# Norm sums by a ones matrix, unit 1's weights in tiles of their own, scaled chunks in PSUM, low parts on GpSimd, squares added in pairs

## The chip, the cores and the metric

One core of a Trainium2 chip. The metric is the device time of one launch in microseconds, median of three runs.

## The reference

A decoder of three layers on one sequence of 512 tokens with 1024 features, in float32. What the change touches is the sequence of RMS norms between the parts:

```python
mixed = jnp.concatenate([y, m_out], axis=-1) @ w_out[l]
h = h + rms_norm(mixed, norm_mix_post[l])
f = swiglu_ffn(rms_norm(h, norm_ffn_pre[l]), w_ffn_in[l], w_ffn_out[l])
h = h + rms_norm(f, norm_ffn_post[l])
```

for l = 0 and 1 (after layer 0's feed-forward `rms_norm(h, norm_kv)` feeds the keys and values). `rms_norm(x, g)` is `x * rsqrt(mean(x * x) + 1e-6) * g`, with the mean over the 1024 features. A third layer follows: a recurrent and Fourier mixer, a post norm, and a mixture of 16 experts.

## The kernel before

The residual stream X lies in SBUF as 8 chunks of 128 features by 512 tokens. A product in float32 is made as three passes in a reduced float32 format: weights and activations are split into a high part (a copy that rounds) and a low part (the difference), and `three_pass` issues high x high, high x low and low x high, each a matmul with 512 columns. `stream` walks over units of two halves (s = 0, 1) of 128 x 1024 weights: SP loads a half into `ring[s]`, ScalarE makes its high part (`split_high`, L221), VectorE the low part (`split_low`, L227), TensorE multiplies. A slot s of `wh`/`wl` is free when the product that read it is done (`used_done`). Rings 2 and 3 carry the modulation weights that GpSimd's queue loads (L189) and VectorE sums up beside the feed-forward (L263).

A layer's output product (`rows_products`) collects all 8 output chunks in the 8 PSUM banks, bank c for chunk c; in its last half TensorE ends them one by one. `rows_root` copies bank 0 to SBUF (`kept`), squares the chunks on ScalarE, adds six of the squares on VectorE, sums over the partitions by matmuls with one column of ones (four token blocks for each of three parts, `roots[:, 0, 0:4]`), takes root and reciprocal of 128 x 4, and spreads the result over the partitions again (`spread_passes`, L525) into bank 0. The first weights of the next product are split on the way. A feed-forward's output lacks one factor, the root of the norm in front of it; so behind a feed-forward the small constant under the root is replaced by a 128 x 4 tile made from that norm's sums (`root_floor`).

`Residual.chunks` then runs over the 8 chunks: VectorE scales chunk k out of its bank (`scale`), adds it to X, ScalarE makes the high part of the next norm's input (times `next_gain`, without its root) and the square, VectorE the low part, and TensorE multiplies the chunk with unit 0 of the next weights (`one_pass`, L654, banks 0 and 1), and sums the square over the partitions by four one-column matmuls (`sum_tokens`). `stream(fused=...)` calls this in place of unit 0; then unit 1's weights are split into the same two slots, `fused.root()` takes the root, unit 1 is multiplied, `fused.spread()` spreads the root to `rstd_t` behind its first half, and the units are evacuated with it. Engines run their own queues in program order; `Queue.do` (L69) issues an instruction that counts its line up, so L69 stands for most of them in the profile.

The chain occurs at five seams: mixer output to feed-forward in layers 0 and 1, layer 0's feed-forward to keys and values (all three with a fused unit 0), layer 1's feed-forward to the norm of the third layer (`norm2`), and the third layer's mixer output to its norm (`norm3`).

## Time and profile before

| | |
|---|---|
| runs | 1956.45, 1950.61, 1950.71 us |
| median | 1950.71 us |
| profiled execution: first to last instruction (span) | 1947.3 us |
| mean granted TensorE clock | 0.950 |
| TensorE busy | 1814.3 us (93%) |
| VectorE busy | 1216.2 us (62%) |
| ScalarE busy | 896.1 us (46%) |
| GpSimd busy | 125.7 us (6%) |
| chain that ended last | PE 85%, DVE 7%, ACT 6% |

Busy is the time in which an engine works on something; the span is the profiled execution's own time between its first and its last instruction, and what lies around it is not in the trace. The granted clock is 1.0 at 2.4 GHz and 0.5 at 1.2 GHz. The chain is followed back from the last instruction to what released each step.

### The profile page before, as it was taken

To read this page: it belongs to the slowest core of one execution; us is meant where nothing else is said; L and a number is where in the kernel's file an instruction comes from. 1 tells how busy PE (TensorE), PEld (TensorE's weight loads), DVE (VectorE), ACT (ScalarE), POOL (GpSimd) and SP (SyncE) were. 2 spreads that over 40 slices of the span, in tenths; PEclk is the share of its full clock that TensorE was granted. 3 is DMA by queue.
4 is the path that set the end of the run, shared out by engine and by line. 5 is a ranking of instruction groups with operands and counts; after the bars stand their busy time and mean duration, and the time that the engine had idled before them with its cause. 6 is when DMAs were issued, how large, how long until landed. Compare 5 with 4: busy or idle time off the path is not lost.

```text
span 1947.3 us, 25641 instructions
## 1 busy us (share of the span) xinstructions
PE 1814.3 (93%) x9201; PEld 1507.9 (77%) x9201; DVE 1216.2 (62%) x2170; ACT 896.1 (46%) x1452; POOL 125.7 (6%) x137
## 2 busy tenths in 40 slices
PE   7997999999999997899999999799987989999997
PEld 7875788888887865678888888678576878888885
DVE  3554668887323656456865532564575479889888
ACT  3446443222213445543223221342383368888885
POOL 1000000000000000000110000120000210110102
PEclk8898999999999998999999999799998879999999
DMA  4223225455333124024655423330011359999995
GB/s 150 87 76 115 87 64 142 134 145 147 107 96 96 44 65 184 23 65 137 182 159 149 119 93 97 112 89 22 21 67 66 108 222 377 395 385 370 386 372 187
DMA packets 203854, 289.32 MB, mean 149 GB/s; under 512 B 12332, under 2 KB 150548, under 8 KB 203636
## 3 DMA queue, kind: packets, MB, share of 16 engines
q1 hardware_dynamic: 188788, 239.56, 36.9%
q0 software_dynamic: 11920, 36.48, 6.1%
q10 hardware_dynamic: 3056, 12.06, 1.6%
q8 instruction: 59, 0.97, 0.2%
q14 instruction: 31, 0.25, 0.0%
HBM read 271.77 MB, written 21.53 MB: 151 GB/s over the span
## 4 chain that ended last, share of the span: by engine, by line
PE 85%; DVE 7%; ACT 6%; issue 1%; DMA 1%; POOL 0%; DVEq 0%; ACTq 0%; POOLq 0%
PE bank L200 23%; PE bank L202 23%; PE bank L201 23%; PE bank L69 11%; PE bank L654 2%; DVE weights_low L227 1%; PE bank L2195 1%; ACT weights_high L221 1%; DVE tmp L69 1%; DVE z_and_u L69 1%; DVE ring L69 1%; PE bank L1651 1%; ACT spare L69 1%; PE bank L2544 1%; PE bank L272 1%
## 5 line engine op out<-in xcount | busy, mean ns | idle before, releaser
L227 DVE TENSOR_TENSOR weights_low<-ring,weights_high 128x1024 fp32r<-128x1024 f32 x202 | 246.7, 1223 | 395.3 <-ACT weights_high L221 394.8
L200 PE MATMUL bank<-XH,weights_high 128*128 128x512 f32 x1056 | 423.2, 401 | 17.8 <-DVE weights_low L227 6.5
L202 PE MATMUL bank<-XH,weights_low 128*128 128x512 f32 x1056 | 415.6, 394 | 0.0
L201 PE MATMUL bank<-XL,weights_high 128*128 128x512 f32 x1056 | 415.2, 393 | 0.0
L221 ACT CAST weights_high<-ring 128x1024 fp32r<-128x1024 f32 x202 | 211.1, 1047 | 432.6 <-PE bank L202 422.8
L200 PEld LDWEIGHTS bank<-XH,weights_high 128*128 128x128 f32 x1056 | 200.8, 190 | 63.0 <-DVE weights_low L227 9.6
L202 PEld LDWEIGHTS bank<-XH,weights_low 128*128 128x128 f32 x1056 | 200.7, 190 | 43.4
L201 PEld LDWEIGHTS bank<-XL,weights_high 128*128 128x128 f32 x1056 | 201.1, 190 | 40.3 <-issue 0.5
L2235 DVE TENSOR_TENSOR XL<-ring,XH 128x1024 fp32r<-128x1024 f32 x144 | 169.8, 1219 | 11.7 <-ACT XH L2229 11.7
L2229 ACT CAST XH<-ring 128x1024 fp32r<-128x1024 f32 x144 | 145.2, 1048 | 0.6 <-PE bank L202 0.6
L69 DVE SCALAR_TENSOR_TENSOR squares<-ring,c_silu,squares 128x128 f32<-128x128 f32 x384 | 135.2, 352 | 13.6
L200 PE MATMUL bank<-hidden_high,weights_high 128*128 128x512 f32 x352 | 137.1, 390 | 0.0
L202 PE MATMUL bank<-hidden_high,weights_low 128*128 128x512 f32 x352 | 137.0, 389 | 0.0
L201 PE MATMUL bank<-hidden_low,weights_high 128*128 128x512 f32 x352 | 136.9, 389 | 0.0
L189 POOL DMA_DIRECT2D ring<-in_w_ada x48 | 42.5, 885 | 711.9 <-DVE squares L263 711.9
L2235 DVE TENSOR_TENSOR weights_low<-ring,weights_high 128x1024 fp32r<-128x1024 f32 x72 | 86.0, 1216 | 0.0
L1196 ACT ACTIVATE tmp<-tmp 128x512 f32<-128x512 f32 x44 | 27.8, 632 | 109.2 <-DVE tmp L1192 109.1
L202 PEld LDWEIGHTS bank<-hidden_high,weights_low 128*128 128x128 f32 x352 | 66.1, 188 | 13.8
L201 PEld LDWEIGHTS bank<-hidden_low,weights_high 128*128 128x128 f32 x352 | 66.1, 188 | 13.8
L200 PEld LDWEIGHTS bank<-hidden_high,weights_high 128*128 128x128 f32 x352 | 66.1, 188 | 13.4
L200 PE MATMUL bank<-weights_high,gathered_high 128*128 128x256 f32 (+1 forms) x216 | 70.8, 328 | 3.6 <-DVE weights_low L2235 1.8
L2229 ACT CAST weights_high<-ring 128x1024 fp32r<-128x1024 f32 x72 | 74.1, 1053 | 0.0
(506 smaller groups left out, 3263.2 us busy)
## 6 DMA issues: line engine op xcount, KB each, us to landing
ring<-in_w_ffn_in SPq DMA_DIRECT2D x88, 512.0 KB, 4.7
ring<-in_w_gate SPq DMA_DIRECT2D x72, 512.0 KB, 5.4
ring<-in_w_up SPq DMA_DIRECT2D x72, 512.0 KB, 7.3
ring<-in_w_down SPq DMA_DIRECT2D x72, 512.0 KB, 5.9
ring<-in_w_ada POOLq DMA_DIRECT2D x48, 512.0 KB, 4.7
ring<-in_w_ffn_out SPq DMA_DIRECT2D x44, 512.0 KB, 3.6
ring<-in_w_out SPq DMA_DIRECT2D x24, 512.0 KB, 3.6
slot_output<-expert_out SPq DMA_DIRECT2D x18, 512.0 KB, 6.7
```

The lines of the kernel that those rows point to most:

```text
L69: op(*args, **kw).then_inc(self.line.sem, 1)
L189: queue.eng.dma_start(dst, src).then_inc(ln.sem, 16)
L200: PE.matmul(out_ap, w_h, x_h, start=first, stop=False, skip_group_check=True)
L201: PE.matmul(out_ap, w_h, x_l, start=False, stop=False, skip_group_check=True)
L202: return PE.matmul(out_ap, w_l, x_h, start=False, stop=last, skip_group_check=True)
L221: S.copy(wh[:, s, :], ring[s][:, :]).then_inc(high_done.sem, 1)
L227: V.tensor_tensor(wl[:, s, :], ring[s][:, :], wh[:, s, :].bitcast(F32), ALU.subtract).then_inc(split_done.sem, 1)
L272: t = PE.matmul(bank[7][:, 2 * n + j:2 * n + j + 1], ada_acc(n, j), ones[:, 0:1], start=True, stop=True, skip_group_check=True)
L654: return PE.matmul(bank[s][:, cols], w[:, s, k * P:(k + 1) * P], x[:, k, cols], start=start, stop=stop, skip_group_check=True)
L1196: S.activation(sg, sg, ACT.Silu).then_inc(silu_done.sem, 1)
L2229: S.copy(high[s], raw[q]).then_inc(l_high.sem, 1)
L2235: V.tensor_tensor(low[s], raw[q], high[s].bitcast(F32), ALU.subtract).then_inc(l_split.sem, 1)
```

## The change

1. `rows_root` sums each of its three parts with one matmul of 128 x 128 ones by 512 columns, so that every partition of bank 0 holds the sum; root and reciprocal are taken of 128 x 512 into `rstd_t`; the spreading is gone. The floor of a feed-forward output is no longer a 128 x 4 tile but a 128 x 512 part (in `spare`) that enters VectorE's chain of additions as one more term. Both splits of the next weights' first halves stand in `rows_root` right behind their high parts.
2. `Early`: unit 1's weights of each feed-forward are loaded into rings 2 and 3 during the mixer output before, and split into tiles of their own. The first modulation loads of each feed-forward move behind that. In `stream`, unit 1 reads those tiles, and unit 2's halves are split in place of unit 1's while unit 1 is multiplied. Waits on slots name the slot's own split.
3. `Transition` replaces `Residual` at the three fused seams: scaled chunks from chunk 2 on are written back to their PSUM bank; squares of odd chunks go to `spare` or to PSUM, VectorE adds each to the even chunk's square, and four sums (ones matrix, or by token at the keys' seam) take the place of eight; the low parts of chunks 0, 1, 2, 4, 5 and 6 are made by a whole copy on ScalarE and a subtraction on GpSimd; TensorE multiplies the low part of a chunk behind the high part of the next. Its root is of 128 x 512 (by token at the keys' seam).

The core of the diff:

```diff
+        class Early:
+            def load(self, *after):
+                sp.need(*after)
+                for s in range(2):
+                    ap, view = self.src(self.unit, s)
+                    load(sp, landed[2 + s], view(ring[2 + s][:, :]), ap)
+
+            def split(self, s, *after):
+                act.need(*after)
+                S.wait_ge(landed[2 + s].sem, landed[2 + s].n)
+                S.copy(self.high[:, s, :], ring[2 + s][:, :]).then_inc(self.high_line.sem, 1)
+                self.high_line.n += 1
+                V.wait_ge(self.high_line.sem, self.high_line.n)
+                V.tensor_tensor(self.low[:, s, :], ring[2 + s][:, :], self.high[:, s, :].bitcast(F32),
+                                ALU.subtract).then_inc(self.split_line.sem, 1)
...
                     elif fused and i == 1:
                         if s == 0:
-                            fill_half(src, i, 0)
-                            fill_half(src, i, 1)
+                            if not early:
+                                fill_half(src, i, 0)
+                                fill_half(src, i, 1)
                             fused.root()
...
+                    elif early and i == 1:
+                        PE.wait_ge(early.split_line.sem, s + 1)
+                        products(i, s, False, early).then_inc(used_done.sem, 1)
...
                             for both in range(2):
+                                if early:
+                                    open_half(src, both, 2)
                                 evacuate(0, both, used_done.n - 2)
...
-            squares = (sq[:, 0, :], sq[:, 1, :], tmp[:, 0, :], spare[:, 1, :])
+            base, used, total = chunk_done.n - (KC - 1), used_done.n, spare[:, 1, :]
+            squares = (sq[:, 0, :], sq[:, 1, :], tmp[:, 0, :], tmp[:, 1, :])
...
+                if c == 0 and floor:
+                    added[c] = vec.do(V.tensor_tensor, total, total, squares[0], ALU.add, after=[squared[0]])
...
-                for t in range(TT):
-                    tok = pe.do(PE.matmul, bank[0][:, t:t + 1], part[:, t * P:(t + 1) * P], ones[:, 0:1],
-                                start=n + t == 0, stop=n == 2, skip_group_check=True)
...
+                tok = pe.do(PE.matmul, bank[0][:, :], ones[:, :], part, start=n == 0, stop=n == 2, after=[ready])
+            bias = {} if floor else {"bias": epsilon[:, 0:1]}
+            t = act.do(S.activation, rstd_t[:, :], bank[0][:, :], ACT.Sqrt, scale=1.0 / D, after=[tok], **bias)
             bank_free[0] = [t]
...
-            return spread_passes(0, 0, t)
+            return vec.do(V.reciprocal, rstd_t[:, :], rstd_t[:, :], after=[t])
...
+                def square(k):
+                    dst = second[k] if k % 2 else sq[:, k // 2 % 2, :]
+                    squared[k] = act.do(S.activation, dst, X[:, k, :], ACT.Square,
+                                        after=[*x_ready[k], *([summed[k - 4]] if k in (4, 6) else [])])
+
+                def pair(k):
+                    paired[k] = vec.do(V.tensor_tensor, sq[:, k // 2 % 2, :], sq[:, k // 2 % 2, :], second[k + 1], ALU.add,
+                                       after=[squared[k], squared[k + 1]])
...
+                def lows(k):
+                    if k in (3, last):
+                        V.wait_ge(act.line.sem, high[k][1])
+                        low[k] = vec.do(V.scalar_tensor_tensor, XL[:, k, :], X[:, k, :], self.next_gain[:, k:k + 1],
+                                        XH[:, k, :].bitcast(F32), ALU.mult, ALU.subtract)
+                    else:
+                        whole = whole_of[k % 4]
+                        act.do(S.activation, whole, X[:, k, :], ACT.Copy, scale=self.next_gain[:, k:k + 1],
+                               after=[low[k - 4]] if k >= 4 else [])
+                        G.wait_ge(act.line.sem, act.line.n)
+                        low[k] = pool.do(G.tensor_tensor, XL[:, k, :], whole, XH[:, k, :].bitcast(F32), ALU.subtract)
...
+                for k in range(1, KC):
+                    if k < last:
+                        scale(k + 1)
+                    add(k)
+                    highs(k)
+                    lows(k)
+                    square(k)
+                    if k % 2:
+                        pair(k - 1)
+                    PE.wait_ge(act.line.sem, high[k][1])
+                    for s in range(2):
+                        one_pass(s, wh, XH, k)
+                        one_pass(s, wl, XH, k)
+                    if k < last:
+                        pe.need(low[k - 1])
+                        for s in range(2):
+                            one_pass(s, wh, XL, k - 1)
+                        if k in (3, 5):
+                            sums(k - 3)
+                sums(last - 3)
+                for s in range(2):
+                    for k in (last - 1, last):
+                        pe.need(low[k])
+                        done = one_pass(s, wh, XL, k, stop=k == last)
+                    done.then_inc(used_done.sem, 1)
+                slots_used(0, 1)
+                sums(last - 1)
...
+            if i == 3:
+                early.split(s, used_done.now())
...
+        early = Early("first_ffn", ffn_src(0), 1, unit_high, unit_low)
+        early.load(used_done.now())
+        rooted = mix_out(I["w_out"][0], ffn_src(0), row_order, row_ready, row_part)
+        G.wait_ge(early.split_line.sem, 2)
         modulation_load(0)
         modulation_load(1)
...
+        def split_early(i, s):
+            if i == 2:
+                early.split(s, used_done.now())
```

## Rows read from the trace of the kernel before

**Rows 1.** The page: the engine TensorE, and the chain that ended last.

```profile
PE 1814.3 (93%) x9201; PEld 1507.9 (77%) x9201; DVE 1216.2 (62%) x2170; ACT 896.1 (46%) x1452; POOL 125.7 (6%) x137
...
PE 85%; DVE 7%; ACT 6%; issue 1%; DMA 1%; POOL 0%; DVEq 0%; ACTq 0%; POOLq 0%
```

**Rows 2.** Windows: length, busy time of each engine, TensorE's clock, DMA.

```profile
262.70:277.30 14.60, 13.79 (x57) 11.03 (x57) 4.90 (x8) 4.29 (x7) 0.00 (x0) 0.88 0.26 73
270.70:276.18 5.48, 5.48 (x27) 4.41 (x25) 2.31 (x4) 4.08 (x5) 0.00 (x0) 1.00 0.01 3
```

**Rows 3.** Timeline of TensorE at the first seam: start, length, instruction, idle before.

```profile
235.62 1.31 PE L69 MATMUL bank<-ones,tmp 128*128 128x1 f32 x8
237.58 2.05 PE L69 MATMUL bank<-const_tables,roots 128*128 128x128 f32 x8 [0.66 <-DVE roots L69]
241.98 0.55 PE L654 MATMUL bank<-XH,weights_high 128*128 128x256 f32 x1 [2.34 <-DVE tmp L69]
```

**Rows 4.** Timeline of VectorE at the first seam.

```profile
239.67 0.75 DVE L69 SCALAR_TENSOR_TENSOR tmp<-spare,columns,bank 128x512 f32<-128x512 f32 x1 [1.12 <-PE bank L69]
```

**Rows 5.** Timelines of TensorE and VectorE at seams B and D.

```profile
625.76 1.03 PE L69 MATMUL bank<-ones,tmp 128*128 128x1 f32 x8
...
628.75 0.75 DVE L69 SCALAR_TENSOR_TENSOR tmp<-spare,columns,bank 128x512 f32<-128x512 f32 x1 [0.20 <-PE bank L69]
...
1241.74 1.03 PE L69 MATMUL bank<-ones,tmp 128*128 128x1 f32 x8
...
1245.66 0.75 DVE L69 SCALAR_TENSOR_TENSOR tmp<-spare,columns,bank 128x512 f32<-128x512 f32 x1 [1.12 <-PE bank L69]
```

**Rows 6.** Timeline of one chunk inside unit 0 of the first seam.

```profile
252.69 0.74 DVE L69 SCALAR_TENSOR_TENSOR tmp<-bank,columns,rstd 128x512 f32<-128x512 f32 x1
...
252.81 0.72 ACT L69 ACTIVATE XH<-X,columns 128x512 fp32r<-128x512 f32 x1 [0.90 <-DVE X L69]
...
253.44 0.61 ACT L69 ACTIVATE spare<-X 128x512 f32<-128x512 f32 x1
253.56 0.75 DVE L69 SCALAR_TENSOR_TENSOR XL<-X,columns,XH 128x512 fp32r<-128x512 f32 x1
...
254.23 0.68 DVE L69 TENSOR_TENSOR X<-X,tmp 128x512 f32<-128x512 f32 x1
...
254.84 0.74 DVE L69 SCALAR_TENSOR_TENSOR tmp<-bank,columns,rstd 128x512 f32<-128x512 f32 x1
```

**Rows 7.** Timeline of TensorE: first products of units 1 and 2 in A, values in B.

```profile
262.71 0.50 PE L200 MATMUL bank<-XH,weights_high 128*128 128x512 f32 x1 [0.31 <-DVE weights_low L227]
...
277.23 0.50 PE L200 MATMUL bank<-XH,weights_high 128*128 128x512 f32 x1 [0.81 <-DVE weights_low L227]
...
653.26 0.55 PE L200 MATMUL bank<-weights_high,XH 128*128 128x256 f32 x1 [1.76 <-DVE weights_low L227]
```

**Rows 8.** Groups by form: busy us, mean ns of one, idle before, releaser.

```profile
L69 DVE RECIPROCAL swa_small<-swa_small 128x4 f32<-128x4 f32 x12 | 2.1, 178 | 0.4
...
L69 DVE RECIPROCAL mem_small<-mem_small 128x4 f32<-128x4 f32 x8 | 1.4, 171 | 0.0
L69 DVE TENSOR_SCALAR mem_small<-mem_small 128x4 f32<-128x4 f32 x8 | 1.4, 170 | 0.3
...
L69 DVE RECIPROCAL out_root<-out_root 128x1 f32<-128x1 f32 x4 | 0.7, 164 | 1.3 <-ACT out_root L69 1.3
...
L69 DVE TENSOR_TENSOR bank<-bank,const_tables 128x512 f32<-128x512 f32 x8 | 5.6, 695 | 10.5 <-PE bank L69 10.5
...
L69 POOL TENSOR_TENSOR squares<-squares 128x512 f32<-128x512 f32 x2 | 3.4, 1708 | 162.8 <-ACT squares L69 162.8
...
L2647 PE MATMUL bank<-ring,const_tables 128*128 128x512 f32 x16 | 7.5, 592 | 0.0
```

**Rows 9.** Timeline of ScalarE at the end of the first mixer output.

```profile
228.39 1.05 ACT L221 CAST weights_high<-ring 128x1024 fp32r<-128x1024 f32 x1 [4.39 <-PE bank L202]
```

**Rows 10.** Timeline of VectorE at seam D, with GpSimd adding.

```profile
1250.62 0.98 DVE L69 TENSOR_TENSOR X<-X,tmp 128x512 f32<-128x512 f32 x1
```

**Rows 11.** Windows in the attention of layer 1, columns as in rows 2.

```profile
764.00:768.00 4.00, 2.34 (x18) 1.54 (x16) 3.93 (x19) 3.61 (x13) 0.00 (x0) 1.00 0.00 0
768.70:772.00 3.30, 3.30 (x32) 3.28 (x32) 1.06 (x4) 2.29 (x10) 0.00 (x0) 0.50 0.00 0
```

More of the change, by code:

```diff
@@ L229, in split_low, with slots_used, wait_slots, __init__ @@
             split_done.n += 1
+            slot_split[s] = split_done.n
+        def slots_used(*each):
+            for s in each:
+                used_done.n += 1
+                slot_used[s] = used_done.n
+        def wait_slots(*each):
+            PE.wait_ge(split_done.sem, max(slot_split[s] for s in each))
+        class Early:
+            def __init__(self, name, src, unit, high, low):
+                self.src, self.unit, self.high, self.low = src, unit, high, low
+                self.high_line, self.split_line = line(f"{name}_high_done"), line(f"{name}_split_done")
+            def load(self, *after):
[11 more added lines that the diff above has]
+                                ALU.subtract).then_inc(self.split_line.sem, 1)
+                self.split_line.n += 1
         def fill_half(src, i, s):
@@ L288, in opener, with stream @@
             return lambda s: open_half(src, s)
-        def stream(units, src, products, evacuate=None, side=None, then=None, fused=None, beside=None, paired=None):
+        def stream(units, src, products, evacuate=None, side=None, then=None, fused=None, beside=None, paired=None, early=None):
             pending = []
@@ L338, in stream @@
                             pending.append(n)
-                            if n + 2 < 48:
+                            if n + 2 < 48 and n + 2 not in (20, 21):
                                 modulation_load(n + 2)
@@ L379, in columns_products, with products @@
         def columns_products(n, xh, xl, to=0, ready=None):
-            def products(i, s, first):
-                w_h = wh[:, s, :].rearrange("p (k n) -> p k n", k=KC)
-                w_l = wl[:, s, :].rearrange("p (k n) -> p k n", k=KC)
+            def products(i, s, first, halves=None):
+                high, low = (halves.high, halves.low) if halves else (wh, wl)
+                w_h = high[:, s, :].rearrange("p (k n) -> p k n", k=KC)
+                w_l = low[:, s, :].rearrange("p (k n) -> p k n", k=KC)
                 b = to + 4 * (i % 2) + s
@@ L393, in columns_products, with token_products @@
             return products
-        def token_products(tiles, xh, xl, to=0, between=None):
+        def token_products(tiles, xh, xl, to=0, between=None, early=None):
             for a in range((tiles + 1) // 2):
                 pe.need(*bank_free[to + a])
-            PE.wait_ge(split_done.sem, used_done.n + 2)
+            if early:
+                PE.wait_ge(early.split_line.sem, 2)
+            else:
+                wait_slots(0, 1)
+            w_h, w_l = (early.high, early.low) if early else (wh, wl)
             for m in range(tiles):
@@ L409, in token_products @@
             last.then_inc(used_done.sem, 2)
-            used_done.n += 2
+            if early:
+                used_done.n += 2
+            else:
+                slots_used(0, 1)
         def rows_products(units, xh, xl, ready=None, order=None, tokens=None, between=None):
@@ L599, in chunks @@
             def chunks(self):
-                order = range(KC)
                 squares = (sq[:, 0, :], sq[:, 1, :], spare[:, 1, :])
-                scaled, summed, low, squared, routed, paired = {}, {}, {}, {}, {}, {}
-                pairs = self.router is None and self.next_gain is None
+                scaled, summed, squared, routed, paired = {}, {}, {}, {}, {}
+                pairs = self.router is None
                 square = [squares[h] for h in ((0, 1, 2, 1, 0, 1, 2, 1) if pairs else (0, 1, 2, 0, 1, 2, 0, 1))]
@@ L621, in token_sums @@
+                    if j:
+                        bank_free[j] = [scaled[j]]
                 def token_sums(src, first):
@@ L635, in sum_tokens @@
                             summed[j] = token_sums(square[j], False)
-                    elif not self.router:
-                        pe.need(squared[j])
-                        summed[j] = token_sums(square[j], j == 0)
                     else:
@@ L734, in root @@
                            bias=epsilon[:, 0:1], after=[self.summed])
-                if self.keep_floor:
-                    t = vec.do(V.tensor_scalar, root_floor[:, :], bank[2][:, 0:TT], EPS / D, EPS * EPS, ALU.mult, ALU.add,
-                               after=[t])
                 bank_free[2] = [t]
@@ L1460, in program @@
         row_ready = {c: outputs_done[5] for c in range(KC)}
-        spread = mix_out(I["w_out"][1], ffn_src(1), row_order, row_ready)
+        unit_high, unit_low = (QL[:, 4 * n:4 * n + 4, :].rearrange("p c t -> p (c t)").rearrange("p (s n) -> p s n", s=2)
+                               for n in range(2))
+        early = Early("second_ffn", ffn_src(1), 1, unit_high, unit_low)
+        early.load(used_done.now(), (ada_summed, ada_sums[19]))
+        def split_early(i, s):
+            if i == 2:
+                early.split(s, used_done.now())
+        root_table()
+        rooted = mix_out(I["w_out"][1], ffn_src(1), row_order, row_ready, split_early)
+        G.wait_ge(early.split_line.sem, 2)
+        modulation_load(20)
+        modulation_load(21)
         b_ctx.close()
```

236 lines of the change are left out of this document (120 added, 116 removed).

## The prediction

> **What bounds the kernel now.** I read the page first: TensorE sets 85% of the chain that ended last, over a span of 1947.3 us [rows 1]. So the change pays only where TensorE stands idle, runs at half clock, or does work that can go. I call the seams that it touches A (mixer output to first feed-forward, from 233.7 us), B (first feed-forward to keys, 623.9), C (mixer output to second feed-forward, 852.8), D (second feed-forward to the norm behind it, 1239.8) and E (last mixer output, 1535.2). Everything outside them is the same code.
>
> Then the windows: in A the second fused unit (unit 1) takes 14.5 us at a mean clock of 0.88, though the 24 passes that start in a stretch of 5.48 us at full clock need 0.228 us each [rows 2]. 48 passes would be 10.95 us, so unit 1 loses about 3.6 us, 1.75 of them by the clock (0.12 of 14.6). The timeline shows the idle time ahead of unit 0: the last token sum ends at 236.93, the eight small spreading passes run from 237.58 to 239.63, and the first product starts at 241.98 [rows 3]; between these VectorE scales chunk 0 from 239.67 [rows 4] and chunk 1 behind it, and the product waits for the latter. In B and D the sums end at 626.79 and 1242.77 and chunk 0 is scaled at 628.75 and 1245.66 [rows 5]; C behaves as B (1.88 us), E too (1.89), D as A (2.89, the spreading at half clock). Inside unit 0 (20.73 us in A, from 241.98 to 262.71 [rows 3, 7]), VectorE scales a chunk every 2.15 us and ScalarE makes high part and square between [rows 6]: both are nearly as full as TensorE. Behind it come waits for split weights: 0.31 us before unit 1, 0.81 before unit 2, and 1.76 behind unit 0 of B [rows 7].
>
> The sum is made against the span of 1947.3 us; the median of the runs is 1950.71, so 3.4 us lie outside it and are carried over.
>
> **1. Root on all 512 columns (five seams).** The 12 one-column matmuls become three of 512 columns. One of those is two records; sixteen records of such a form have a mean of 592 ns [rows 8] and start 0.43 us apart, so 0.86 us a part against 0.88 now: no change. Root, reciprocal of 4, spreading go; a root of 512 comes (0.60, as a square of 512 columns takes 0.61 [rows 6]), a reciprocal of 512 and 0.15 us of handovers. The reciprocal of 512 has no row. Below, it is a plain pass of 512, 0.69 us. Above, I take the slope from 164 ns for one column to 178 for four (swa_small), 4.7 ns a column: 2.55 us. I take 0.70, since on the same tile four columns cost 171 ns as a reciprocal and 170 as a tensor_scalar [rows 8], which leaves no room for several cycles per column. So from end of sums to chunk 0: 1.45 us, against 2.74 (A), 1.96, 1.88, 2.89, 1.89: gain 1.29 + 0.51 + 0.43 + 1.44 + 0.44 = 4.1 us. The page VectorE: DVE Perf Modes of the Trainium skill (the 8-slice pipeline) says that reciprocal runs divide steps with a repeat count of 8; read as eight cycles an element at its 0.96 GHz that is an estimate of 4.3 us for 512 columns, and the change would then come out about 18 us worse than by my value. The row of four columns speaks against that reading. After feed-forwards (B, D) one more addition heads VectorE's chain of sums; the total is then ready at about 625.75, when TensorE comes free of the second part at 625.7, so it costs nothing, but has no slack left.
>
> **2. Weights split early.** Unit 1 has its own tiles, split during the mixer output, a stage that TensorE sets. SP issues the two loads before the mixer rows, in place of two loads that GpSimd issued then: the same bytes, so I cost it at nothing. In C both splits end well before the seam. In A the second one waits, at i = 3, for the product before last, that is until 228.39, the very moment when the root's first split starts now [rows 9]. Behind it on ScalarE stand that split (1.05 us) and the squares, and on VectorE its low part (1.22) stands before the copy of bank 0 and so before the whole chain of additions. Followed through with those durations, chunk 7's square ends 1 us later than now and the sums at 237.7 instead of 236.93. Cost 0.8 us, in A alone; if the slack were better than I think, 0.
>
> **3. Unit 0 rewritten (A, B, C).** VectorE loses six low parts (0.67 between starts each), gains four pair sums. ScalarE gains six copies of 0.72. GpSimd makes six low parts at 1.7 us [rows 8], less than the time between chunks, so they hide; uncovered, each would cost its 1.7. TensorE drops four of eight token-sum groups. But the order on the queues couples two engines. VectorE's pair sum of an odd chunk waits for that chunk's square, the last of ScalarE's three works, and the next scale and addition stand behind it; ScalarE meanwhile has nothing. A work is followed by the next 0.63 us after its start when it is a high part or a whole copy (252.81 to 253.44 [rows 6]), and about 0.54 when it is a square. With t from the first product: addition 1 ends at 1.3, square 1 at 3.2, then pair, scale, addition: addition 2 ends at 5.2. Chunks 2 and 3 end their squares at 8.25 and the low part of 3 at 8.55, addition 4 ends at 10.4, square 5 at 14.1, addition 6 at 16.1, high part 7 at 18.65. TensorE then still has four passes, a 512-wide sum, four passes, a last sum: 0.9 + 0.86 + 0.9 + 0.86, so 22.25. TensorE's own work (48 passes, four sums: 14.4 us at full clock) fits in it. Writing scaled chunks to PSUM is free: VectorE from bank to bank is 695 ns [rows 8]. While GpSimd adds, VectorE's additions of two SBUF tiles take 0.98 us, not 0.69 [rows 10]; pair 0 and low part 3 meet this on the path: 0.3 each. Unit 0 comes to 22.85 us, between 20.7 (the present length, if the coupling hid) and 24.5 (half clock in the tail, whose 3.5 us would double in part).
> Now: 20.73 in A (from 241.98 to 262.71) and as much in C (20.63); loss 2.1 and 2.2. In B unit 0 and the wait behind it are 22.2 now. The splits of the value weights start when half 0's last pass ends; the token sum between the halves goes, so that this pass comes about 0.6 us closer to the end, and the wait of 1.76 us [rows 7] becomes about 2.25: 22.85 + 2.25, loss 2.9. Sum: 7.2 us lost.
>
> **4. Unit 1.** With weights ready and no spreading passes, unit 1 can run its 48 passes in 10.95 us, and unit 2's weights are split by 8.1 us after its start. Against 14.5 now, gain 3.56 in A and in C: 7.1 us. This needs full clock. Now unit 1 has 0.88 in the mean, behind a tail of one-column sums; the new tail is 3.5 us of wide work. If the clock falls anyway I lose 1.7 us a seam.
>
> **Sum.** -4.1 + 0.8 + 7.2 - 7.1 = -3.2 us: span 1944.1, median **1947.5 us**.
>
> **Rivals.**
> - *Reciprocal slow.* 1.85 us more in each of five seams, 9.3 us: 1956.8, slower. It decides once the reciprocal costs over 1.35 us, where the sum is nought. For it: the growth from one to four columns; against: the two equal rows. 0.13.
> - *Clock falls inside unit 0.* TensorE is busy about 60% of the time from t = 10 to t = 18. In attention, 4 us at 2.34 busy stood at clock 1.00 and were followed by 3.3 us at 0.50 [rows 11]. A fall here would put tail or unit 1 at half clock in A, B, C: 3 x 1.7 = 5.1: 1952.6, no change. 0.24.
> - *The coupling hides.* If square and pair sum overlap more than the order suggests, unit 0 keeps its 20.7 us or less: 2.15 us back in each, 6.4 us: 1941.1, faster. For it: the sum of ScalarE's work is only 14.5 us in all. 0.22.
> - *No effect*, i.e. unit 1 again waits, for its root instead: then about 1951, 0.05.
> - My forecast with its own neighbourhood, 1945 to 1950: 0.36.
>
> A measurement of this kernel can tell 0.3%, 5.9 us. The forecast lies inside it, and so do the clock and the no-effect case in the main: same 0.45. Faster (the hidden coupling and the lower edge of the forecast) 0.32; slower (reciprocal, or clock and long unit 0 together) 0.23. The range goes from 1940.5 to 1957; the forecast's own is 1944 to 1951.
>
> **What would show it.** A 512-wide reciprocal of about 0.7 us, and chunk 0 scaled 1.45 us behind the sums. In unit 0, gaps of about 2 us in ScalarE before the high parts of chunks 2, 4 and 6, each ended by VectorE, and unit 0 two microseconds longer. No wait in front of units 1 and 2 of A and C. In B a wait of 2.2 us for weights_low. In A squares that start 1.6 us later. I am wrong if the reciprocal is long, if the granted clock is half at the end of unit 0, or if GpSimd's low parts take over 2.5 us and TensorE waits for them.

## The result: 1970.2 us, 1% slower, and the profile after

The changed kernel takes 1970.2 us (median of 4 runs, 1968.5 to 1973.6), the kernel before beside it 1950.97 (4 runs). The ratio is 1.0094, 95% interval 1.007 to 1.0118: slower, outside my range of 1940.5 to 1957. The execution that was profiled is the slowest of the four (1973.6).

The page of the changed kernel, engines and chain, against [rows 1]:

```profile
PE 1804.8 (92%) x8911; PEld 1471.9 (75%) x8911; DVE 1235.9 (63%) x2164; ACT 904.0 (46%) x1463; POOL 150.5 (8%) x155
...
PE 81%; DVE 9%; ACT 7%; issue 2%; DMA 1%; POOL 0%; ACTq 0%; DVEq 0%; POOLq 0%
```

TensorE works 9.5 us less, and yet the span is 24.8 us longer (1972.1): VectorE's share of the chain went from 7% to 9%, TensorE's from 85% to 81%. The group of the reciprocals by form: five are those of `rows_root`, two those of `Transition`'s own root in A and C. Below it, VectorE at seam A, against [rows 4]:

```profile
L69 DVE RECIPROCAL rstd<-rstd 128x512 f32<-128x512 f32 x7 | 23.5, 3353 | 12.3 <-ACT rstd L69 12.3
```

```profile
240.86 3.35 DVE L69 RECIPROCAL rstd<-rstd 128x512 f32<-128x512 f32 x1 [0.91 <-ACT rstd L69]
244.25 0.75 DVE L69 SCALAR_TENSOR_TENSOR tmp<-spare,columns,rstd 128x512 f32<-128x512 f32 x1
...
249.83 1.28 DVE L69 TENSOR_TENSOR squares<-squares,spare 128x512 f32<-128x512 f32 x1 [1.99 <-ACT spare L69]
...
270.31 3.35 DVE L69 RECIPROCAL rstd<-rstd 128x512 f32<-128x512 f32 x1 [3.26 <-ACT rstd L69]
```

TensorE at the same seam, against [rows 3, 7] (last part of the sums, first product of unit 0, last sum, first product of units 1 and 2):

```profile
239.08 1.02 PE L69 MATMUL bank<-spare,ones 128*128 128x512 f32 x2
...
246.68 0.55 PE L783 MATMUL bank<-XH,weights_high 128*128 128x256 f32 x1 [6.58 <-DVE tmp L69]
...
268.54 1.02 PE L69 MATMUL bank<-squares,ones 128*128 128x512 f32 x2
268.99 0.80 PE L200 MATMUL bank<-XH,next_unit_high 128*128 128x512 f32 x1
...
280.59 0.39 PE L200 MATMUL bank<-XH,weights_high 128*128 128x512 f32 x1
```

The reciprocal of 512 columns is 3.353 us, not 0.70: the wait before the first product went from 2.34 to 6.58 us. Units 0 and 1 together went from 35.25 us (241.98 to 277.23) to 33.91, and no wait stands in front of units 1 and 2 any more: the second reciprocal of A (270.31) runs beside unit 1 and costs nothing there.

Both profiled executions, cut at the same instructions, give this table: length now minus length before, in us, and what the prediction's steps say of it.

| stage | measured | predicted |
|---|---|---|
| start to the mixer's last projection scaled out before A (same code) | +2.45 | 0 |
| A: from there to the end of sums | +0.72 | +0.8 |
| end of sums to first product, A / B / C | +1.53 / +2.22 / +2.40 | -1.29 / -0.51 / -0.43 |
| end of sums to chunk 0, D / E | +1.17 / +2.25 | -1.44 / -0.44 |
| first product to first modulation sum, A / C | -1.50 / -1.36 | -1.46 / -1.36 |
| B: first product to values | +4.28 | +2.9 |
| B: values to next projections | +1.14 | 0 |
| both feed-forward output products | +3.48, +3.48 | 0 |
| attention (same code) | -2.12 | 0 |
| experts to the last root | +2.74 | 0 |
| the rest | +1.95 | 0 |

The first line is the clock: TensorE's matmuls step at full clock from 24.9 us on before and from 34.1 on now, in code that the change does not touch; a part of that is made up again by 73 us, where the kernel before is at half clock for longer. The rows of the chunks' coupling come out as forecast in A and C, not in B. The roots are each 2.6 to 2.8 us worse than forecast. And 9.7 us lie in the two output products and the experts' stage, of which the prediction does not speak. ScalarE inside unit 0 of A:

```profile
249.11 0.61 ACT L69 ACTIVATE spare<-X 128x512 f32<-128x512 f32 x1
252.40 0.72 ACT L69 ACTIVATE XH<-X,columns 128x512 fp32r<-128x512 f32 x1 [2.68 <-DVE X L69]
...
257.55 0.72 ACT L69 ACTIVATE XH<-X,columns 128x512 fp32r<-128x512 f32 x1 [2.19 <-DVE X L69]
...
263.20 0.72 ACT L69 ACTIVATE XH<-X,columns 128x512 fp32r<-128x512 f32 x1 [2.08 <-DVE X L69]
```

Three gaps of 2.1 to 2.7 us before the high parts of chunks 2, 4 and 6, each ended by VectorE, which itself had waited for ScalarE's square (1.99 us at 249.83).

The feed-forward output products are the same instructions in both kernels, in the same order, at clock 1.00, with no wait. First and last of 71 successive matmuls before (70 steps in 15.86 us: 0.2266 us), TensorE's timeline:

```profile
607.63 0.39 PE L201 MATMUL bank<-hidden_low,weights_high 128*128 128x512 f32 x1
...
623.49 0.39 PE L202 MATMUL bank<-hidden_high,weights_low 128*128 128x512 f32 x1
```

and of 78 in the changed kernel (77 steps in 17.97 us: 0.2334 us; over all 528 the mean steps are 0.2267 and 0.2333):

```profile
612.22 0.40 PE L200 MATMUL bank<-hidden_high,weights_high 128*128 128x512 f32 x1
...
630.19 0.40 PE L202 MATMUL bank<-hidden_high,weights_low 128*128 128x512 f32 x1
```

Each such product has 528 of them: 528 x 0.0067 = 3.5 us, the line of the table. What differs is where the tiles lie. The removed tile `root_floor` took 32 bytes of each partition, so every tile declared behind it (hidden, projections, the experts' tiles) begins 32 bytes lower; X, XH and the weights' slots are declared ahead of it and did not move.

### The profile page after: what moved, and what is told of

The parts are those of the page before. It is cut to its first block, busy times and chain, and to the rows that moved or that the text cites. A ratio compares the mean times of both kernels' runs of the same rounds, so it can differ in the third digit from the quotient of the medians.

```text
span 1972.1 us, 25103 instructions
## 1 busy us (share of the span) xinstructions
PE 1804.8 (92%) x8911; PEld 1471.9 (75%) x8911; DVE 1235.9 (63%) x2164; ACT 904.0 (46%) x1463; POOL 150.5 (8%) x155
## 4 chain that ended last, share of the span: by engine, by line
PE 81%; DVE 9%; ACT 7%; issue 2%; DMA 1%; POOL 0%; ACTq 0%; DVEq 0%; POOLq 0%
PE bank L200 23%; PE bank L202 23%; PE bank L201 22%; PE bank L69 10%; PE bank L2324 1%; DVE weights_low L226 1%; DVE X L69 1%; ACT XH L69 1%; DVE tmp L69 1%; DVE rstd L69 1%; ACT tmp L69 1%; ACT squares L69 1%; DVE squares L69 1%; ACT spare L69 1%; ACT weights_high L220 1%
## 5 line engine op out<-in xcount | busy, mean ns | idle before, releaser
L226 DVE TENSOR_TENSOR weights_low<-ring,weights_high 128x1024 fp32r<-128x1024 f32 x198 | 241.8, 1224 | 392.3 <-ACT weights_high L220 391.9
L200 PE MATMUL bank<-XH,weights_high 128*128 128x512 f32 x1024 | 409.8, 400 | 15.5 <-DVE XL L69 5.7
L220 ACT CAST weights_high<-ring 128x1024 fp32r<-128x1024 f32 x198 | 207.0, 1048 | 433.6 <-PE bank L202 425.8
L202 PE MATMUL bank<-XH,weights_low 128*128 128x512 f32 x1024 | 402.8, 393 | 0.0
L201 PE MATMUL bank<-XL,weights_high 128*128 128x512 f32 x1024 | 402.1, 393 | 0.0
L200 PEld LDWEIGHTS bank<-XH,weights_high 128*128 128x128 f32 x1024 | 194.6, 190 | 58.0 <-issue 7.6
L202 PEld LDWEIGHTS bank<-XH,weights_low 128*128 128x128 f32 x1024 | 194.3, 190 | 41.7
L201 PEld LDWEIGHTS bank<-XL,weights_high 128*128 128x128 f32 x1024 | 194.8, 190 | 39.2 <-issue 0.5
L2364 DVE TENSOR_TENSOR weights_low<-ring,weights_high 128x1024 fp32r<-128x1024 f32 x72 | 86.1, 1218 | 0.0
L2358 ACT CAST weights_high<-ring 128x1024 fp32r<-128x1024 f32 x72 | 74.1, 1053 | 0.2 <-PE bank L202 0.2
```

The source lines that it names most:

```text
L200: PE.matmul(out_ap, w_h, x_h, start=first, stop=False, skip_group_check=True)
L201: PE.matmul(out_ap, w_h, x_l, start=False, stop=False, skip_group_check=True)
L202: return PE.matmul(out_ap, w_l, x_h, start=False, stop=last, skip_group_check=True)
L220: S.copy(wh[:, s, :], ring[s][:, :]).then_inc(high_done.sem, 1)
L226: V.tensor_tensor(wl[:, s, :], ring[s][:, :], wh[:, s, :].bitcast(F32), ALU.subtract).then_inc(split_done.sem, 1)
L2358: S.copy(high[s], raw[q]).then_inc(l_high.sem, 1)
```

## The experiments

All kernels from here on keep the number of the last expert block (at most 22) in five bits. The edit of that, and of the first kernels:

```diff
+        last_block = nc.snap(last_block & 31, engines=[...], min_val=0, max_val=BLOCKS - 1)
```

**Control.** Nothing but that.

> Control. The changed kernel as it is, but the number of the last expert block (at most 22) is masked with 31 in a register of each engine before the experts; the other kernels have this too. Every theory: the time of the changed kernel, 1970 us, give or take 2, ratio to the kernel before 1.010.

1972.3 us, ratio 1.0128 (1.0109 to 1.0147): the changed kernel's time within the intervals. In its profiled execution the first line of the table is +0.63 us and not +2.45; every other stage is within 0.1 us of the changed kernel's. So the table's other lines are no chance of the changed kernel's one execution. The execution of the kernel before that they are compared with can still be one: see B's values and the experts below.

**The 32 bytes back, in the changed kernel.**

```diff
         probe = sbuf("sqrt_probe", [1, 1])
+        sbuf("pad", [P, 8])
```

> The changed kernel with a tile of 32 bytes a partition, which nothing uses, where the small tile root_floor stood before it was removed; so every tile declared behind it is back at its old address (hidden_high0 from byte 138336 to 138368, which is 1081 times 128). Theory address: in both feed-forward output products the step from one matmul to the next is 0.2333 us in the changed kernel and 0.2267 before, 528 matmuls each; it goes back to 0.2267, 7.0 us less, and the experts' stage gives back 1 to 3 us more: 1960 to 1962 us. Rival clock or chance (the step belongs to the run, or to the DMA traffic beside it, not to the address): no change, 1970.

1962.3 us, ratio 1.0063 (1.005 to 1.0077): 0.0065 of 1951, that is 12.7 us or (by the medians) 10.0 us less than the control. Both feed-forward output products are back at 122.6 us (125.99 and 126.06 without the tile), step 0.2267; that is 7 us, and the address it is. The experts' stage is 2.2 us shorter too, but it was at half clock for 8.7 us in this execution and for 12.1 us in the control's, so the address is not shown to be the cause there.

**The same shift in the kernel before.** The same line of code.

> The kernel before with a tile of 32 bytes, unused, behind sqrt_probe; nothing else is changed but the addresses of all tiles declared later (hidden_high0 from byte 138368 to 138400). Theory address: both feed-forward output products step at 0.2333 instead of 0.2267, 7.0 us more, and the experts' stage 1 to 3 us more: 1958 to 1961 us, ratio 1.0035 to 1.0055. Rival clock or chance: no change, 1951.

1958.0 us, ratio 1.0045 (1.0027 to 1.0062), 8.8 us: a tile that nothing uses makes the kernel before slower by half of what the whole change did. Its output products took 125.98 and 126.05 us, with a step of 0.2333; the experts' stage only 0.4 us more; the attention stage was 3.4 us shorter in that execution, the other way. (This kernel has the five bits of the last block as well. No run has them alone in the kernel before; the next one has them and is at 1.0008.)

**A shift of 64 in the kernel before** (`[P, 16]` in place of `[P, 8]`).

> The kernel before with 64 unused bytes a partition behind sqrt_probe, in place of the 32 of the shift before. hidden_high0 then begins at 1081.5 times 128 bytes, a multiple of 64 but not of 128; x_high_b, which stood at 1338.5 times 128 and whose products step at 0.2334 us in the kernel before, comes to a multiple of 128. Theory 128: hidden products at 0.2333 (7 us more), products of x_high_b at 0.2267, about 1 us less: 1954 to 1957 us. Rival 64: a multiple of 64 is enough, hidden products stay at 0.2267, then no change, 1949, and the 0.2334 of x_high_b has another cause.

Ratio 1.0008 (0.9997 to 1.002), and neither theory was right: the hidden products step at 0.2289 us, between the two, and those of `x_high_b` (the tokens for the projections behind B) went from 0.2334 to 0.228. The experts' products stepped at 0.2295 us instead of 0.2327, and their stage was 4.0 us shorter (at 4.1 us less of half clock), against 2.8 us more in the hidden products. So a multiple of 128 is not the rule; the rule is measured by itself below.

**A copy for the reciprocal.**

```diff
-            return vec.do(V.reciprocal, rstd_t[:, :], rstd_t[:, :], after=[t])
+            return vec.do(V.tensor_copy, rstd_t[:, :], rstd_t[:, :], after=[t])
```

> The changed kernel with the five reciprocals of 128x512 in rows_root replaced by a copy of the same tile (so the norms multiply by the root in place of its inverse: that part of the computation is changed). Theory price: the reciprocal is 3.353 us each and all of it stands on the path; a copy of 512 columns should take 0.6 to 0.7, so 5 x 2.7 = 13.4 us go: 1957 us. Rival hidden: part of the 3.35 us covers something else (the splits behind it), then less than 10 us go. If my own sum of the other parts had been right, this kernel would be at 1947.5; address theory says that 7 to 10 us above this remain.

1940.8 us, but this total can't be read: with other values in the norms the experts had fewer blocks (816 matmuls read `gathered_high` instead of 864), and the stage from the experts' first product to the last root took 327.8 us where the control took 348.0. Up to the third norm the comparison holds. From the end of sums to chunk 0 the five seams took 1.22, 1.13, 1.22, 1.13 and 1.27 us instead of 4.15, 4.06, 4.15, 4.06 and 4.15: 14.6 us, the difference of 3.353 to a copy's 0.43 five times. All of the reciprocal of `rows_root` lies on the path. At the third norm's root only 9.3 us of it were to be seen (1568.86 against 1578.11), since stages of unchanged code were longer in this execution, attention by 3.1 and the third layer's mixer by 1.3.

**One-column sums and spreading again, 32 bytes back.** The core of it:

```diff
-                tok = pe.do(PE.matmul, bank[0][:, :], ones[:, :], part, start=n == 0, stop=n == 2, after=[ready])
+                pe.need(ready)
+                for t in range(TT):
+                    tok = pe.do(PE.matmul, bank[0][:, t:t + 1], part[:, t * P:(t + 1) * P], ones[:, 0:1], ...)
...
+            t = vec.do(V.reciprocal, roots[:, 0, :], roots[:, 0, :], after=[t])
+            return spread_passes(0, 0, t)
```

> The changed kernel with the 32 bytes back (the second experiment), and rows_root's end as before the change: one-column sums, root and reciprocal of 128x4, spreading by TensorE, at all five seams. Theory price: from the end of sums to chunk 0 the five seams take 4.15 us each with the reciprocal of 512, and 2.74, 1.96, 1.88, 2.89 and 1.89 before; 9.4 us go from 1962.3: 1953 us. Rival: if a slow reciprocal was only hidden behind the splits of the next weights, the splits now stand on the path and less than 5 us go: 1957 or more.

1959.9 us, ratio 1.0032 (1.0021 to 1.0043): 0.0031 less than with the wide root, 6.0 us with some 3 us of uncertainty, and not 9.4. The five stages from sums to chunk 0 took 2.74, 2.34, 2.74, 2.65 and 1.89 us, together 8.2 less than with the wide root (4.15, 4.06, 4.15, 4.06, 4.15). In C the eight spreading passes took 2.04 us as in A [rows 3], and not 1.1 as in E. That is the clock, and the kernel before has it too: its C took 1.88 us in the profile of the prediction, and 2.74 in those of the last two experiments on it below, whose code is the same up to there. At A the sums ended 1.6 us later. So the wide root is a loss of some 6 to 8 us. With 8.2 us over five seams it breaks even at a reciprocal of 3.353 - 1.64 = 1.7 us, and with 6.6 us (less the 1.6 at A) at 2.0, both estimates.

**Pair sums one chunk later, 32 bytes back.**

```diff
-                    if k % 2:
-                        pair(k - 1)
+                    if k in (2, 4, 6):
+                        pair(k - 2)
+                    if k == last:
+                        pair(last - 1)
```

> The changed kernel with the 32 bytes back, and in the fused unit 0 each pair sum but the last issued one chunk later on VectorE (behind the next chunk's addition and not in front of its scaling). Theory coupling: the pair sum in program order ahead of the next scale and addition makes ScalarE stand idle 2.2 to 2.7 us three times in each unit 0 (22.9 us at A and C, 24.0 at B); with the pair sum later these gaps close and unit 0 falls to 20.0 to 21.0 us in A and C, as much less in B: 6 us less in all, 1956 us. Rival: ScalarE is simply full (four works a chunk), unit 0 stays above 22.3 us: 1961 to 1962.

1951.5 us, ratio 0.9996 (0.9985 to 1.0007): 13 us less than with the 32 bytes alone by the ratios (10.7 by the medians), twice what I expected. Unit 0 of A took 18.35 us, less than the 20.73 of the kernel before. ScalarE inside unit 0 of A in this kernel:

```profile
251.83 0.72 ACT L69 ACTIVATE XH<-X,columns 128x512 fp32r<-128x512 f32 x1 [0.94 <-DVE X L69]
...
254.63 0.72 ACT L69 ACTIVATE XH<-X,columns 128x512 fp32r<-128x512 f32 x1 [1.58 <-DVE X L69]
```

The gaps are 0.94 and 1.58 us now, and the third is gone. The stretch from the first product to the first modulation sum is 46.3 us in A and 46.1 in C against 50.3 and 50.1, and B's from first product to values 21.2 against 26.5. In B there was a second loss. Windows of the changed kernel over the end of B's unit 0, columns as in [rows 2]:

```profile
655.00:657.00 2.00, 0.80 (x9) 0.71 (x7) 2.00 (x4) 0.52 (x1) 0.29 (x1) 1.00 0.00 0
657.00:659.00 2.00, 1.75 (x6) 1.23 (x7) 0.06 (x2) 2.00 (x5) 1.11 (x1) 0.79 0.00 0
659.00:661.00 2.00, 2.00 (x7) 1.61 (x6) 1.33 (x2) 0.43 (x1) 0.17 (x1) 0.50 0.00 0
661.00:663.00 2.00, 2.00 (x13) 1.88 (x12) 0.00 (x0) 0.13 (x1) 0.00 (x0) 0.85 0.00 0
```

and of the kernel with the late pairs over the same work:

```profile
642.00:647.00 5.00, 4.81 (x26) 3.52 (x24) 2.91 (x6) 4.77 (x9) 3.83 (x3) 1.00 0.00 0
647.00:649.00 2.00, 2.00 (x14) 1.82 (x14) 1.32 (x2) 0.43 (x1) 0.00 (x0) 1.00 0.00 0
649.00:651.00 2.00, 1.80 (x12) 1.54 (x12) 0.28 (x1) 1.36 (x2) 0.41 (x1) 1.00 0.00 0
```

TensorE stood half idle (0.80 of 2.00 us busy), then the granted clock fell to 0.50 just as the dense tail began. With the gaps closed it stays at 1.00. The idle stretch in front of the tail alone does not decide it: in the kernel with one-column sums above, TensorE is as idle there (0.86 of 2.00 us busy), but the half clock at the start of B's unit 0 lasted until 647.7, 9.8 us into it instead of 4.5, the middle gap was filled, and the clock did not fall again inside unit 0. It took 25.3 us to the values. So the fall cost about 1.2 us of the 5.3.

**Both edits, and addresses.** One-column sums and late pairs, on top of the 32 bytes, and other starts for the early unit's tiles and `x_high_b`:

```diff
+        sbuf("pad_a", [P, 8], F32, a_ctx)
         unit_high, unit_low = (sbuf(f"next_unit_{x}", [P, 2, HALF], F32R, a_ctx) for x in ("high", "low"))
...
+        sbuf("pad_b", [P, 16], F32, b_ctx)
         QH, QL = sbuf("x_high_b", [P, KC, T], F32R, b_ctx), sbuf("x_low_b", [P, KC, T], F32R, b_ctx)
```

> The two edits before together, and x_high_b, x_low_b and the tiles of the early unit begun at multiples of 128 bytes (64 and 32 unused bytes in front of them). If the theories add up: 1962.3 - 9.4 - 6 - 1.5 for the addresses = 1945.4 us, ratio 0.9985 to the kernel before. If only the reciprocal's share is right: 1951 to 1953.

1944.0 us, ratio 0.996 (0.9944 to 0.9976): faster than both kernels, by 7.8 us against the kernel before. The ratios measured one by one add up: 1.0063 - 0.0031 - 0.0067 - 0.0008 for the addresses = 0.9957. The 0.9985 that I expected lies outside the interval, since it counted 15.4 us for the two edits where their ratios give 19.

**Early splits at the third pair of halves**, in the first mixer output, on top of that.

```diff
-            if i == 3:
+            if i == 2:
                 early.split(s, used_done.now())
```

> The kernel of the two edits and the addresses together, with the early unit's splits in the first mixer output at its third pair of halves (i = 2) and not the fourth. Theory: at A the second early split waits for a product that ends 4 us before the end of the mixer output and holds up the root's split, the squares and the sums by 0.65 us against the kernel before with the wide root and by 2.2 us with one-column sums; these go: 1942 us, ratio 0.995. Rival: the one-column sums themselves are late and slow there (half clock), the splits are not the cause: no change from 1944.

The stage up to the end of A's sums took 50.05 us, where the kernel before has 50.08, the changed kernel 50.80 and the previous one 52.30: what holds the sums up is the second early split. The total does not show the 2 us that I expected: 1945.9 us, ratio 0.996 (0.9946 to 0.9975), the same as without. In the profiled execution the second mixer output began at half clock and took 57.4 us instead of 53.4, which the kernel before shows too in the profile of the last experiment (57.3).

**The two prices by themselves.** The kernel before, and behind its end the following:

```diff
+        for n in (1, 4, 8, 16, 32, 64, 128, 256, 512):
+            for _ in range(2):
+                t = vec.do(V.reciprocal, two[:, 0:n], one[:, 0:n], after=[t])
...
+        for w_at, x_at in [(0, 0), (0, 32), ...]:
+            for k in range(6):
+                for a, b in ((0, 0), (0, 1), (1, 0)):
+                    w0, x0 = w_at // 4 + k * P, x_at // 4 + k * T
+                    PE.matmul(bank[0][:, :], w_flat[a][:, w0:w0 + P], x_flat[b][:, x0:x0 + T], ...)
```

> The kernel before, and behind its end a measurement: on VectorE reciprocals of 128 rows by 1, 4, 8, 16, 32, 64, 128, 256 and 512 columns, a copy and a product of 512; on TensorE 24 groups of 18 matmuls (128x128 by 512, high and low tiles in turn as in the products), with the weights' and the moving tile's start moved by 0 to 224 bytes from where both are multiples of 128. Theory slope: the reciprocal takes about 6.3 ns a column beyond a fixed part of 0.13 us, so 64 columns 0.53, 256 columns 1.74 us, 512 columns 3.35 us; rival, a step between 4 and 512 columns: then short ones stay near 0.17 to 0.2 us up to some width. Theory 128: the step is 0.2267 us when both starts are multiples of 128, 0.2333 us when one is off by 32 or 96, about 0.229 when by 64; weights count as the moving tile does. Rival moving: only the moving tile's start counts, the groups with moved weights stay at 0.2267.

The groups of VectorE by form (out of 128 rows; busy, mean ns):

```profile
L69 DVE RECIPROCAL tmp<-tmp 128x512 f32<-128x512 f32 x2 | 6.7, 3353 | 0.1
L69 DVE RECIPROCAL tmp<-tmp 128x256 f32<-128x256 f32 x2 | 3.5, 1753 | 0.1
L69 DVE RECIPROCAL tmp<-tmp 128x128 f32<-128x128 f32 x2 | 1.9, 953 | 0.1
L69 DVE TENSOR_TENSOR tmp<-tmp 128x512 f32<-128x512 f32 x2 | 1.4, 692 | 0.1
L69 DVE RECIPROCAL tmp<-tmp 128x64 f32<-128x64 f32 x2 | 1.1, 553 | 0.1
L69 DVE COPY tmp<-tmp 128x512 f32<-128x512 f32 x2 | 0.9, 427 | 0.1
...
L69 DVE RECIPROCAL tmp<-tmp 128x16 f32<-128x16 f32 x2 | 0.5, 253 | 0.1
...
L69 DVE RECIPROCAL tmp<-tmp 128x8 f32<-128x8 f32 x2 | 0.4, 203 | 0.1
L69 DVE RECIPROCAL tmp<-tmp 128x4 f32<-128x4 f32 x2 | 0.4, 178 | 0.1
L69 DVE RECIPROCAL tmp<-tmp 128x1 f32<-128x1 f32 x2 | 0.3, 164 | 0.1
```

A straight line from 4 columns on: 153 ns and 6.25 ns a column. At 4 columns the slope's part is 25 ns of 178.

The groups of matmuls begin at these rows of TensorE's timeline, for instance (weights and tokens both off by 64, then both by 96):

```profile
2042.00 0.47 PE L2698 MATMUL bank<-XH,weights_high 128*128 128x512 f32 x1
...
2046.30 0.48 PE L2698 MATMUL bank<-XH,weights_high 128*128 128x512 f32 x1
```

and (tokens alone off by 96, then by 128):

```profile
1984.64 0.48 PE L2698 MATMUL bank<-XH,weights_high 128*128 128x512 f32 x1
...
1989.08 0.48 PE L2698 MATMUL bank<-XH,weights_high 128*128 128x512 f32 x1
```

4.30 us against 4.44 for the same 18 matmuls and the small one between groups. The table has the mean step from the fourth to the last matmul of a group, good to some 0.0005 us; the difference is the start of the moving tile minus the start of the weights, modulo 256 bytes. The very first group ran partly at half clock and is left out; the last repeats it. All of it is one execution.

| difference | step, us |
|---|---|
| 0 (both off by 0, 32, 64, 96, 128) | 0.2271, 0.2279, 0.2271, 0.2279, 0.2286 |
| +64 (moving off 64; weights off 192) | 0.2293, 0.2286 |
| +32, +224 (two groups each) | 0.2336, 0.2336; 0.2329, 0.2329 |
| +96, +160 (two each) | 0.2343, 0.2336; 0.2343, 0.2343 |
| +128, +192 (two each) | 0.2321, 0.2321; 0.2329, 0.2336 |
| +4; +16; +240; +252 | 0.2386; 0.2321; 0.2264; 0.2321 |

So neither theory was right: no tile's own alignment counts, but how they lie to each other. Equal starts modulo 256 are fast wherever both are, +64 is at their slow end, and of the others only 16 bytes less (240, one group) is as fast. This also explains the shift of 64, whose hidden products have a difference of +64 and x_high_b of 0.

**The addresses everywhere**, on top of all edits above:

```diff
-        sbuf("pad_a", [P, 8], F32, a_ctx)
+        sbuf("pad_a", [P, 40], F32, a_ctx)
...
+        sbuf("pad_e", [P, 32], F32, e_ctx)
         hgh, hgl = sbuf("gathered_high", [P, KC, P], F32R, e_ctx), sbuf("gathered_low", [P, KC, P], F32R, e_ctx)
```

> The kernel with late pairs, one-column sums, earlier split and addresses, and now also 128 unused bytes in front of the experts' gathered_high and 160 in place of 32 in front of the early unit's tiles. The measurement showed that what counts is the difference of the two operands' starts modulo 256: 0 gives 0.2264 to 0.2286 us a step, plus 64 gives 0.229, all others 0.232 to 0.239. The experts' products now have weights and tokens 128 bytes apart (0.2325 us a step); with 0 they should step at 0.2267. Of some 1020 steps' worth of 512 columns that is 6 us if TensorE sets that stage: about 1938 us, ratio 0.993. Rival: the experts' weights arrive no faster than now, the stage is bound by loads: no change from 0.996.

1939.2 us, ratio 0.9947 (0.9933 to 0.9961), 10.3 us faster than the kernel before, where I expected 0.993. The experts' products step at 0.2288 us (0.2322 without), and their stage up to its last product took 325.4 us. Unit 1 of A steps at 0.2275 us now and took 11.3 us; it had 0.2334 us in the changed kernel and 0.2325 in the two kernels before this one.

**In the kernel before alone**, the line with `pad_e`:

> The kernel before with only the 128 unused bytes in front of gathered_high in the experts' stage. Theory difference modulo 256: 5 to 6 us less, 1945 to 1947 if the kernel before is at 1951, ratio 0.997. Rival (loads bound the experts' stage, or multiples of 128 are enough): ratio 1.000.

Ratio 0.9984 (0.9974 to 0.9993), 3.1 us: about half of what I expected. The step fell only to 0.2288, and the experts' stage from 329.2 to 325.5 us, at 3.1 us less of half clock in this execution; the ratio over twelve runs is the surer figure. Products that read XH and XL step at 0.2272 to 0.2278 us, those that read the weights' slots still at 0.229 to 0.235.

## Why the prediction was wrong, step by step

- **What bounds the kernel** held: TensorE's busy time fell and the time rose, since TensorE stood idle for longer at the seams.
- **Step 1 failed**, in the sentence "I take 0.70, since on the same tile four columns cost 171 ns as a reciprocal and 170 as a tensor_scalar [rows 8], which leaves no room for several cycles per column." It leaves room: at four columns 150 ns are a fixed part, and 6.25 ns a column more are 25 ns of the rest. Measured 3.353 us, so 2.65 us more in each of five seams, 13.3 us. This alone takes the forecast of 1947.5 to 1960.8, outside the range. The upper bound of 2.55 was too low as well: a slope from one column to four (4.7 ns) is not that from four on. The page VectorE: DVE Perf Modes of the Trainium skill (the 8-slice pipeline), which I weighed and set aside, pointed the right way: its repeat count read as eight cycles an element gave an estimate of 4.3 us where the trace has 3.353, and the measured 6.25 ns are six cycles at its 0.96 GHz, an estimate too. The rest of step 1 was right: sums about as long as before (0.90 us a part), square root 0.69 us (0.60 forecast). But 1.88 us for C stood on one execution; at half clock the kernel before takes 2.74 there.
- **Step 2** was right: +0.72 us at A for 0.8, and no delay is left when the splits come earlier.
- **Step 3** was right in A and C, its mechanism (VectorE's pair sum behind ScalarE's square) in the gaps of 2.1 to 2.7 us. Unit 0 of A is 22.31 us for 22.85. Its terms were not all right: 18.65 + 0.9 + 0.86 + 0.9 + 0.86 is 22.17 and not 22.25, and of the two terms of 0.3 for GpSimd's additions pair 0 took 0.60 us more and low part 3 nothing, so that their sum was right by luck. The step only compared with the old unit 0; what another order on the queue could reach, 13 us less, it didn't ask. In B the clock rival came true on top: 26.5 us to the values for 25.1, and 25.3 in the kernel whose clock did not fall there. GpSimd's low parts took 1.29 us (the first of each unit 0 took 1.83), not 1.7, and hid.
- **Step 4** had the mechanism right: no wait, full clock, 11.6 us for unit 1 of A where it took 14.52 before. It forecast 10.95; the step is 0.2334 us there, since the early unit's tiles lie badly to XH (0.2275 with equal starts). That units 0 and 1 together came out at -1.50 us for -1.46 is luck: unit 0 was 0.54 us shorter than forecast and unit 1 0.65 us longer.
- **Not in the prediction at all:** the removal of a tile of 4 columns moved all later tiles. 7.0 us in the two output products by count and step. The undoing measured 10.0 us by the medians, the same shift in the kernel before 8.8 (5.3 to 12.1). For the experts' 2.7 us no run shows the address as the cause: 3.1 us lie behind the last product with gathered tokens, where the changed kernel was at half clock for 6.8 us and the kernel before never, and the profile of the measurement, with the addresses of the kernel before, has 2.4 us of them too. No rival held the addresses, and nothing in my range stood for them: they were a term put at nothing with the words "Everything outside them is the same code".

The account: my sum of -3.2, +13.3 for the reciprocal, +10 for the addresses and +1.4 for the clock in B make +21.5 us; measured +19.2 by the medians and +24.8 in the profiled execution. What is left is of the size of what stages of unchanged code do from run to run (attention -2.1, second mixer output up to +3.9 in single executions). That B's values took 1.1 us more is the clock and not the change: in the first 5 us of that stage it is 0.50 in the changed kernel and 0.69 in the kernel before, and two more profiles with the kernel before's code and addresses up to there (the measurement and the last experiment) have 0.50, and 17.8 and 17.9 us against 16.3. Why the products that read the weights' slots gain little from equal starts, and the experts so only half, is open. So is how an address comes to set the step at all.

## What to carry to other kernels

Don't price a wide operation from a narrow one: at 4 columns the fixed 150 ns hide a slope that makes 3.2 us of 512 columns, and where a row for the real width is missing, the range has to hold the slope that the narrow rows can't exclude. On one engine's queue, an instruction that waits for the last work of another engine goes behind the work that this engine needs next; here one chunk later was worth 13 us. Compare with a second execution of the kernel before: here the clock alone moved single stages by 1 to 4 us. When a change adds or removes a tile, compare the starts of all later tiles, and try the two operands of long matmul streams at equal starts modulo 256 bytes.

## What the runs showed of the hardware that was not expected

- VectorE's float32 reciprocal: 153 ns plus 6.25 ns a column from 4 columns on (178 ns for 4, 3353 for 512), where a product of two tiles of 512 takes 692 ns and a copy 427.
- The matmul step of 128x128 by 512 at full clock is 0.227 to 0.229 us with both operands at equal starts modulo 256 bytes, 0.229 with the moving one 64 further, 0.232 to 0.239 at the other differences tried (but 0.2264 with the moving one 16 less). On a kernel of 1951 us an unused tile of 32 bytes was 8.8 us.
- Gaps of 0.9 to 1.7 us in TensorE's work inside one stage were followed by a granted clock of 0.50 at B in the changed kernel (the same in the control and with the 32 bytes back), and by none at A and C, where gaps of 0.9 to 1.6 us stand.
- While GpSimd subtracted (249.28 to 250.56 us in the changed kernel), VectorE's addition of two SBUF tiles took 1.28 us instead of 0.68. Where VectorE's addition began at the same moment (247.16), it took 0.68 us, and GpSimd's subtraction 1.83 instead of 1.29.
